# Sparse attention: the low parts of eight weight units made by GpSimd instead of VectorE

## The reference

```python
s = jnp.einsum('bgrqd,bgcd->bgrqc', qc, kc) + shared_bias(dist)      # compressed keys
p_cmp = masked_softmax(s, dist >= 0)
o_cmp = jnp.einsum('bgrqc,bgcd->bgrqd', p_cmp.astype(vc.dtype), vc)
...
p = masked_softmax(s, (dist >= 0)[:, :, None])                        # selected blocks
o_slc = jnp.einsum('bgrqk,bgqkd->bgrqd', p.astype(vb.dtype), vb)
...
p = masked_softmax(s, mask)                                           # window
o_win = jnp.einsum('bgrqk,bgkd->bgrqd', p.astype(vw.dtype), vw)
...
gate_a, gate_b = jnp.split(merge_g, N_BRANCHES, axis=-1)
m = jax.nn.sigmoid(gate_a) * y_a + jax.nn.sigmoid(gate_b) * y_b
```

## Time and profile before

| | us |
|---|---|
| median of three runs | 2326.83 |
| lowest and highest | 2325.88 to 2328.31 |
| span of the profiled execution | 2325.0 |
| PE busy in it | 2297.9 (99%) |
| PEld busy | 1970.8 (85%) |
| DVE busy | 1642.4 (71%) |
| ACT busy | 1174.8 (51%) |
| POOL busy | 221.3 (10%) |

### The profile page before, as it was taken

How to read it: one execution, slowest core, us unless ns; L and a number is a source line. 1 busy time by engine, 2 the same in 40 slices (tenths; PEclk the granted TensorE clock), 3 DMA queues, 4 the chain that set the end, 5 groups by cost and what they waited for, 6 DMA issues and landing times.

```text
span 2325.0 us, 32912 instructions
## 1 busy us (share of the span) xinstructions
PE 2297.9 (99%) x12127; PEld 1970.8 (85%) x12127; DVE 1642.4 (71%) x2531; ACT 1174.8 (51%) x1901; POOL 221.3 (10%) x343
## 2 busy tenths in 40 slices
PE   8999999999999999999999999999999999999999
PEld 4888888888888998998888887898888887888787
DVE  5886777798688876887686788764333387479874
ACT  5547788723334431342557887343222265567741
POOL 1200000120001112211100000100000001011120
PEclk9999999999999999999999999999999999999999
DMA  7421111283333336447321112523323325422263
GB/s 299 167 67 48 49 39 48 82 301 118 118 129 138 112 109 231 148 142 254 123 80 63 61 49 69 197 84 100 100 91 100 100 100 180 160 99 85 91 217 110
DMA packets 72101, 282.41 MB, mean 121 GB/s; under 512 B 9120, under 2 KB 9184, under 8 KB 70032
## 3 DMA queue, kind: packets, MB, share of 16 engines
q1 hardware_dynamic: 43056, 162.94, 20.7%
q0 software_dynamic: 28896, 117.46, 14.4%
HBM read 245.76 MB, written 33.55 MB: 120 GB/s over the span
## 4 chain that ended last, share of the span: by engine, by line
PE 91%; DVE 3%; ACT 3%; issue 2%; DMA 1%; POOL 0%; SPq 0%; ACTq 0%; DVEq 0%; POOLq 0%
PE ps L218 25%; PE ps L219 25%; PE ps L220 24%; PE ps L1395 2%; PE ps L1468 2%; PE ps L1402 2%; PE ps L1469 2%; PE ps L1470 2%; PE ps L1449 1%; PE ps L846 1%; PE ps L2882 1%; PE ps L1453 1%; PE ps L1029 1%; PE ps L1487 1%; ACT pr L1531 1%
## 5 line engine op out<-in xcount | busy, mean ns | idle before, releaser
L218 PE MATMUL ps<-h_hi,w_hi 128*128 128x512 f32 (+2 forms) x1592 | 573.8, 360 | 2.8 <-DVE h_lo L728 1.1
L219 PE MATMUL ps<-h_lo,w_hi 128*128 128x512 f32 (+2 forms) x1592 | 564.1, 354 | 0.0
L220 PE MATMUL ps<-h_hi,w_lo 128*128 128x512 f32 (+2 forms) x1592 | 563.1, 354 | 0.0
L214 DVE TENSOR_TENSOR w_lo<-w_raw,w_hi 128x1024 fp32r<-128x1024 f32 x256 | 312.6, 1222 | 169.2 <-ACT w_hi L207 168.9
L207 ACT ACTIVATE w_hi<-w_raw 128x1024 fp32r<-128x1024 f32 x256 | 269.2, 1053 | 235.4 <-PE ps L220 218.7
L218 PEld LDWEIGHTS ps<-h_hi,w_hi 128*128 128x128 f32 x1592 | 300.5, 189 | 52.3 <-issue 9.1
L220 PEld LDWEIGHTS ps<-h_hi,w_lo 128*128 128x128 f32 x1592 | 300.0, 188 | 43.8
L219 PEld LDWEIGHTS ps<-h_lo,w_hi 128*128 128x128 f32 x1592 | 300.5, 189 | 41.5 <-issue 2.4
L219 PE MATMUL ps<-q_lo,w_hi 128*128 128x512 f32 x720 | 256.3, 356 | 0.0
L218 PE MATMUL ps<-q_hi,w_hi 128*128 128x512 f32 x720 | 255.5, 355 | 0.0
L220 PE MATMUL ps<-q_hi,w_lo 128*128 128x512 f32 x720 | 254.5, 354 | 0.0
(11 more groups left out here) (462 smaller groups left out, 4243.2 us busy)
## 6 DMA issues: line engine op xcount, KB each, us to landing
w_raw<-in_stream SPq DMA_DIRECT2D x288, 512.0 KB, 3.3
wt_x<-in_ada_t POOLq DMA_DIRECT2D x24, 512.0 KB, 3.8
wt_h<-in_ada_t POOLq DMA_DIRECT2D x20, 512.0 KB, 5.0
wt<-in_ada_t POOLq DMA_DIRECT2D x16, 512.0 KB, 4.5
ada_raw<-in_ada SPq DMA_DIRECT2D x6, 1024.0 KB, 20.9
x_keep<-x POOLq DMA_DIRECT2D x8, 768.0 KB, 8.8
gates<-th_g POOLq DMA_DIRECT2D x16, 384.0 KB, 2.7
gates<-sg POOLq DMA_DIRECT2D x24, 256.0 KB, 2.4
```

Source lines behind the costliest of these rows:

```text
L214: nc.vector.tensor_tensor(w_lo[:, u % 3, :], raw[:, u % 2, :], w_hi[:, u % 3, :].bitcast(F32), ALU.subtract).then_inc(lo_ready, 1)
L218: nc.tensor.matmul(out_ap, lh, rh, start=start, stop=False)
L219: nc.tensor.matmul(out_ap, lh, rl, start=False, stop=False)
L220: return nc.tensor.matmul(out_ap, ll, rh, start=False, stop=stop)
```

## The change

A function `split_lo_pool` is added, which does what `split_lo` does on GpSimd's queue. It waits for the high part, for the unit before (`lo_ready`, u) and, after the subtraction, for its own completion. It is called for every head behind `cmp_scale(i)`, and so ahead of the wait for the gate row and of the two DMAs. VectorE's call at step 6 goes. At the start of the next part VectorE waits for `lo_ready` to reach base + 2, before it makes low parts again.

```diff
+        def split_lo_pool(pool, u):
+
+            pool.wait_ge(hi_ready, u + 1 - 2 * pairs_before(u))
+            pool.wait_ge(lo_ready, u)
+            nc.gpsimd.tensor_tensor(w_lo[:, u % 3, :], raw[:, u % 2, :], w_hi[:, u % 3, :].bitcast(F32), ALU.subtract).then_inc(lo_ready, 1)
+            pool.wait_ge(lo_ready, u + 1)
...
                     if n % 8 == 5:
                         cmp_take(hd)
-                    if n % 8 == 6:
-                        split_lo(e, base + hd + 2)
...
                     cmp_scale(i)
+                    split_lo_pool(e, base + i + 2)
                     e.wait_ge(gated.sem, gated.base + i + 1)
...
+                e.wait_ge(lo_ready, base + 2)
                 for k in range(9):
                     split_lo(e, base + k + 2)
```

## The result

The changed kernel takes 2337.8 us in the median of five runs (2334.91 to 2338.68), the kernel before 2326.83 (2325.88 to 2328.31, by now also of five): a ratio of 1.0039, with an interval of 1.0029 to 1.0050. The profiled execution spans 2336.0 us against 2325.0. The forecast was 2336.2 us, within 2331.5 to 2341.0.

What follows compares the result with a forecast made beforehand. PE, busy 2297.9 of 2325.0 us, was taken as the bound. Head losses 4.29 + 3.52 + 0.95 + 0.89 = 9.65, less 0.28, gave +9.4 on 2326.8: 2336.2 us, range 2331.5 to 2341.0.

Steps and rivals of the forecast that it cites:

- What bounds the kernel: Whole kernel: PE is busy 2297.9 of 2325.0 us, so only its idle time can be gained.
- how little there was to win: Relieving DVE wins 0.28 us before turn(7) in four heads and 0.58 in the last, 0.9 in all.
- The lock on scale(4): Scale(4) on DVE stands still until POOL's subtraction ends, 2.70 us after L3150; its margin before turn(4) is 0.33.
- a faster POOL: POOL's subtraction by the skill's figure: 2.25 us instead of 2.41, making the sum about 1.2 us smaller.
- No slowdown: Rival: DVE isn't held up for this pair, only the gain is left; -0.9, 2326.0 us; chance 0.08.
- faster: Rival, by more than 0.2%: needs 4.7 us of PE idle time caused by the subtraction; 0.9 found; chance 0.03.
- slower than 2.40: Rival: POOL's subtraction takes 0.45 us more in each of eight heads; +14.2, 2341.0 us; chance 0.10.
- The race in heads 3 and 5: POOL starts before DVE's scale(4), at 2104.23 against 2104.29; PE loses 1.76 us a head, 3.52 together.
- The handoff on POOL: From the end of `cmp_scale` (L3150) to the subtraction's start, with three waits: 0.20 us, an estimate.
- Head 0: DVE's scale(4) goes first, POOL holds up scale(5), PE loses 0.95 us; with POOL first it costs 2.13 instead of 0.88.
- The margin of 0.06: POOL's lead in heads 3 and 5; rival, DVE goes first there: 0.51 instead of 1.76, +6.9, 2333.7 us; chance 0.12.
- After a stall PE doesn't catch up: PE in every head: its only other waits are round trips beginning on PE itself, which move along with the stall.

Runs made afterwards that it cites:

- e1_none: The kernel before with DVE's eight subtractions cut to one column and none on POOL; 2325.78 us against 2327.12, ratio 0.9992.
- e7_after_scale: e4_late with one wait more, so POOL's subtraction (heads 0 to 6) starts after scale(7) on DVE; 2326.84 us against 2327.18, ratio 0.9999.
- e5_early: The changed kernel with POOL's subtraction moved ahead of the next head's queries and `cmp_scale`; 2327.25 us, ratio 1.0001 to the kernel before.
- e2_both: The changed kernel with DVE's subtraction put back as well, behind POOL's; 2335.69 us, ratio 1.0040 to the kernel before.
- e3_half: The changed kernel with POOL subtracting only 512 of the 1024 columns, the rest left out; 2327.9 us, ratio 1.0001 to the kernel before.
- e6_memset: The changed kernel with POOL's subtraction replaced by a memset of the same 128x1024; the single run took 2325.55 us.
- e4_late: The changed kernel with POOL's subtraction behind the gate-row and bias DMAs in heads 0 to 6, the last head's on DVE; 2332.1 us, ratio 1.0024.
- e8_best: e7_after_scale with the last head's subtraction also on POOL, ahead of its `cmp_scale`; 2327.52 us, ratio 1.0001 to the kernel before.
- e9_double: The changed kernel with each POOL subtraction made twice, one right behind the other; 2340.9 us, ratio 1.0061 to the kernel before.

## Why the prediction was right

**What bounds the kernel, and how little there was to win:** right. e1_none shows 0.86 us of gain where I had worked out 0.9 (0.28 and 0.58).

**The lock on scale(4) is the whole loss:** right, and shown by moving it away (e7_after_scale 0.0; in e5_early 1.0 is left, 0.9 of it in head 0, where the place has no slack), by keeping only it (e2_both), and by halving it (e3_half). The duration of 2.40 us came out as 2.34 to 2.40, so the 1.2 us of a faster POOL, by which the range was widened, wasn't needed. The scale ends 0.08 to 0.09 after POOL, where I had 0.10. The Trainium skill (SBUF — State Buffer, "Who interferes with whom") says that `tensor_scalar` can run in a mode that needs both pairs of ports and that the second to come stands still for all of the other's instruction; the rows of head 3 agree, and e6_memset agrees that POOL's writing alone is enough.

**No slowdown, and faster:** the two rivals of the good side are refuted by the 2.28 us row in head 3. POOL is not slower than 2.40 either. The race in heads 3 and 5 was won by POOL, as forecast (in head 3 at 2110.08, DVE at 2110.25).

**Steps that were off.** Three small ones:
- The handoff on POOL from `cmp_scale` to the subtraction. I took 0.20 as an estimate for three waits; it is 0.08 (2109.60 + 0.40 to 2110.08). The waits were long since satisfied. In heads 1 to 6 that makes the loss 0.12 smaller each.
- Head 0. I let whoever has the earlier recorded start go first, and gave the ports to DVE for a lead of 0.04. With the true handoff POOL even started 0.08 before DVE; but by e4_late, where a lead of 0.16 didn't do, POOL would probably have won with the handoff of 0.20 as well. The head cost 1.99, not 0.88; that was the variant for which I had 2.13. The margin of 0.06 that worried me in heads 3 and 5 was no risk: POOL started 0.17 and 0.18 before DVE there. The 0.12 on that rival was too much.
- "After a stall PE doesn't catch up" was too strict. In head 3, turn(4) to turn(5) takes 1.60 after instead of 1.71 (2112.58, 2114.18; before 2105.02, 2106.73), and to turn(6) 3.00 instead of 3.06: some 0.2 us of a stall of 1.6 comes back. With the handoff, head 3 costs 1.40 instead of 1.76, head 1 0.67 instead of 0.99, and heads 2, 4 and 6 0.82 each instead of 1.03. Head 7 came out at 0.90 (forecast 0.89).

In sum +9.4 became +8.8: about 1.7 us less in heads 1 to 6, 1.1 more in head 0. That the two nearly cancel is luck, and the sum looks more exact than its terms. The median of the first five runs is +11.0; the 2.2 beyond the stage came, in the profiled execution, from the clock at the start of the span, which no reasoning on the change could give. On the other chip it was +9.1.

**Where I was wrong was e4_late,** by the same step as in head 0: I read recorded starts as the order in which the ports are given, and took a place beside the start of a scale for one behind it. I had also costed POOL's DMAs only as something that the subtraction might delay. The page of the Trainium skill just named, in "SBUF: two separate sides", tells of one direction, in which DVE keeps GpSimd from writing a DMA's descriptors; head 3 of e4_late agrees (a DMA issued 0.02 behind a scale took 0.65 instead of 0.54), and heads 4 and 6 show that it goes the other way too. In e8_best I overlooked something else: the last head's subtraction held a step of the convolution. I had also taken a win of 0.7 in the last head of e5_early from its marks; read at `cmp_shift`, that head lost 0.26.

What stays open: what lies between a lead of 0.16 and one of 0.23, whether 0.16 would do without the DMA just ahead of POOL's subtraction, and why in head 6 the subtraction could go ahead of a scale that was already waiting, when in e9_double the scale got in between two subtractions. There the second one starts 0.08 after the first and not 0.02, and waits for it; a DMA followed by an instruction with a gap of its own, with nothing else changed, wasn't run.

## What to carry to other kernels

An idle engine is not a free engine: before work is moved from VectorE to GpSimd, look at which VectorE instruction with all its data in SBUF (not only the one you watch) starts within GpSimd's duration, and how much slack its reader has; the price is GpSimd's remaining duration less that slack, and an instruction short enough for the slack is free. Ask first what the relieved engine is worth on the path (here 0.86 us of 9.7), since that bounds every version. If it must be moved, let a semaphore of VectorE start it when a scale has ended, rather than trust that it will come a tenth or two later.

## What the runs showed of the hardware

- The order of recorded starts isn't the order in which the two engines go: VectorE's scale lost with a lead of 0.14 and of 0.16 us (each time with a DMA on GpSimd's queue ending 0.01 before the subtraction), and won with 0.23 and more. By an estimate from alone and held durations (0.35 and 0.08, 0.55 and 0.30), what decides comes about 0.26 us after the scale's recorded start.
- Issuing a DMA on GpSimd's queue holds VectorE's scale as well: 0.53 us for 0.48 alone, and 2.99 when a subtraction followed 0.02 behind the DMA (e4_late). The other way round, a DMA issued 0.02 behind a scale took 0.65 us for 0.54.
- Other VectorE instructions with all their data in SBUF are held as well: a step of the convolution took 2.20 us for 0.74 (e8_best), and in the kernel before the last instruction of `cmp_sum` (L3086, at 2067.14) took 0.99 for 0.35 beside `prep`.
- A GpSimd memset of 128x1024, which only writes, takes 0.95 us and holds the scale as the subtraction does: 0.94 and 0.83 us for 0.35 (e6_memset).
- VectorE gets in between two GpSimd instructions that are 0.08 us apart (e9_double).
- Two dependent instructions on GpSimd follow at 0.07 to 0.09 us whether the second has one wait or three, if the waits are already satisfied.
- The granted clock of TensorE stood at 0.87 from 30 to 40 us of the span in one execution of the changed kernel and at 1.00 in another, with 2.0 us between them at the first mark. In one of e5_early it stood at 0.72 there, and the stage began 4.25 us later than before.
